# The even layer's gate and convolution products laid between its attentions' steps, and the first transfers and norm reordered

## The reference, cut to what matters

```python
px = hx @ w_in            # 1024 x 4096: eight parts of 512
qa, ka, va, ga, bb, cb, ub, gb = jnp.split(px, 8, axis=-1)
...
# attention over context and tokens, two maps per head, 8 heads of 64
s = jnp.einsum('bqhmd,bkhmd->bhmqk', q, k).astype(jnp.float32) * (A_QK ** -0.5)
p = jax.nn.softmax(s, axis=-1)
a = p[:, :, 0] - lam * p[:, :, 1]
o = jnp.einsum('bhqk,bkhd->bqhd', a, v.astype(jnp.float32))
...
out_a = diff_attention_post(o, subln, lam_init).astype(px.dtype) * jax.nn.silu(ga)
out_b = short_conv(bb, cb, ub, conv_w) * jax.nn.silu(gb)   # bb * conv3(cb * ub)
out_x = jnp.concatenate([out_a, out_b], axis=-1)
...
x = x + g_x * rms_norm(mx @ w_out[l], norm_post[l])
```

## Time and profile before

| | |
|---|---|
| runs | 1628.0 us median of 3 (1619.35 to 1629.15) |
| the profiled execution | 1629.48 us, its span 1627.7 us, mean granted clock 0.949 |
| PE busy | 1428.6 us (88%) |
| PE weight loads busy | 1145.8 us (70%) |
| DVE busy | 743.7 us (46%) |
| ACT busy | 661.2 us (41%) |
| POOL busy | 433.1 us (27%) |

### The profile page before, as it was taken

One profiled execution on the slowest core, in us unless ns is written; L12 is line 12 of the kernel. 1 busy time (PEld: TensorE's weight loads), 2 busy tenths in 40 slices (PEclk: granted clock), 3 DMA queues, 4 the chain that ended last, 5 costly groups with the idle time before them and its releaser, 6 DMA issues. The chain is left out here.

```text
span 1627.7 us, 20847 instructions
## 1 busy us (share of the span) xinstructions
PE 1428.6 (88%) x7788; PEld 1145.8 (70%) x7788; DVE 743.7 (46%) x1455; ACT 661.2 (41%) x1426; POOL 433.1 (27%) x340
## 2 busy tenths in 40 slices
PE   5999789999999788599899879999795898889986
PEld 4777567776787566586677757888684786777765
DVE  2154875644314222604499887322303603982123
ACT  4435226643422333421477662411224423663323
POOL 2433243430343323122100002323131333112522
PEclk9999899999999899799999989999998899999998
DMA  4212242100333534320000001121222210103341
GB/s 160 85 71 78 104 156 78 53 27 27 130 130 128 195 110 149 117 95 35 26 1 1 2 1 52 52 78 53 85 84 107 87 75 26 47 24 138 122 151 56
DMA packets 23250, 129.98 MB, mean 80 GB/s; under 512 B 2544, under 2 KB 4208, under 8 KB 10608
## 3 DMA queue, kind: packets, MB, share of 16 engines
q1 hardware_dynamic: 16304, 106.10, 18.0%
q10 hardware_dynamic: 6848, 22.55, 3.9%
HBM read 122.35 MB, written 6.29 MB: 79 GB/s over the span
## 5 line engine op out<-in xcount | busy, mean ns | idle before, releaser
L930 POOL TENSOR_TENSOR w_low<-w_raw,w_high 128x512 fp32r<-128x512 f32 x296 | 384.6, 1308 | 1112.7 <-ACT w_high L1017 1112.5
L1017 ACT CAST w_high<-w_raw 128x512 fp32r<-128x512 f32 x296 | 179.2, 620 | 667.9 <-PE psum L564 490.8
L564 PE MATMUL psum<-x_high,w_high 128*128 128x512 f32 (+1 forms) x696 | 285.1, 410 | 18.1 <-DVE k_low L1615 8.9
L564 PE MATMUL psum<-x_low,w_high 128*128 128x512 f32 (+1 forms) x696 | 275.0, 395 | 0.0
L564 PE MATMUL psum<-x_high,w_low 128*128 128x512 f32 (+1 forms) x696 | 274.2, 394 | 0.0
L564 PEld LDWEIGHTS psum<-x_high,w_high 128*128 128x128 f32 (+1 forms) x696 | 132.3, 190 | 59.6 <-issue 26.8
L679 PE MATMUL psum<-k_high,q_masked 128*128 128x256 f32 (+3 forms) x512 | 139.2, 356 | 31.4 <-DVE q_masked L1609 15.6
L564 PE MATMUL psum<-w_high,x_high 128*128 128x512 f32 (+1 forms) x352 | 140.5, 399 | 20.0 <-ACT w_high L1017 12.7
L564 PEld LDWEIGHTS psum<-x_high,w_low 128*128 128x128 f32 (+1 forms) x696 | 131.7, 189 | 30.1
L564 PEld LDWEIGHTS psum<-x_low,w_high 128*128 128x128 f32 (+1 forms) x696 | 132.4, 190 | 21.9 <-issue 0.5
L564 PE MATMUL psum<-w_low,x_high 128*128 128x512 f32 (+1 forms) x352 | 137.8, 391 | 0.0
(11 more groups left out here) (262 smaller groups left out, 2468.3 us busy)
## 6 DMA issues: line engine op xcount, KB each, us to landing
w_raw<-stream SPq DMA_DIRECT2D x98, 1024.0 KB, 4.8
x_kept<-arena ACTq DMA_DIRECT2D x8, 512.0 KB, 4.3
arena<-x_kept ACTq DMA_DIRECT2D x8, 512.0 KB, 6.5
arena<-bias ACTq DMA_DIRECT2D x8, 448.0 KB, 3.3
arena<-rows ACTq DMA_DIRECT2D x6, 512.0 KB, 5.3
arena<-x SPq DMA_DIRECT2D x4, 512.0 KB, 5.2
arena<-x ACTq DMA_DIRECT2D x4, 512.0 KB, 6.0
arena<-ctx ACTq DMA_DIRECT2D x4, 512.0 KB, 4.9
```

The source lines that it names most:

```text
L564: mm = pe.matmul(o, l, r, start=(first and n == 0 and kind != "fc"), stop=(last and n == len(passes) - 1))
L930: pool.tensor_tensor(WL[:, u % ROOM, :], RAW[:, g % 2, u % 4, :], WH[:, u % ROOM, :].bitcast(F32), ALU.subtract).then_inc(w_lo, 1)
L1017: act.copy(WH[:, u % ROOM, :], RAW[:, g % 2, u % 4, :]).then_inc(w_hi, 1)
```

## The change

The five chunks e_ga, cb, ub, bb, gc are cut into 20 small ones of two units: 128 output features by the whole depth (`SLIM`; e_gate, e_c, e_u, e_b, e_last, four tiles each, taken tile by tile). `slim` makes such a chunk as 8 pieces of three matmuls on the tokens (bank 6), then 8 on the context (bank 7). PE runs both attentions as one loop over 48 steps (and three to finish), with `feed_even` at four places of each step: after each map's scores, after the first four transposes, and at the end; 320 pieces over 180 feeds, the last at step 44. Transposes now have bank 4 alone, values bank 5. ACT and DVE take each finished part in `fed_even`, one step later: ACT between its two exponentials, DVE between the normalization and its second maximum. ACT copies all transposed tiles, also in "dc". The convolution's output is kept in merge_a's room, the gates in b_high's and b_low's.

After the attentions, ACT and DVE split the six convolution tiles, then DVE squares, takes the reciprocals tile by tile in a new order, and multiplies the gate right behind; then the attention's six tiles are split. The rows of the output weights are rolled, so that the convolution half comes first in eo0. The order of the gate rows, of their transfers and of eo0 is unchanged.

At the start SP sends cols and the identity behind the x tiles, then two granules, then the other constants. ACT waits for cols before the first square and takes one root per tile; DVE scales each tile at once; PE transposes a tile when it comes, over eight banks. ACT's copies of masks and its sigmoid of the condition come after the weights of "keys".

```diff
+SLIM = ("e_gate", "e_c", "e_u", "e_b", "e_last")
...
-    + [("e_q", 8), ("e_k", 8), ("e_v", 8), ("e_ga", 8), ("cb", 8), ("ub", 8), ("bb", 8), ("gc", 8)]
+    + [("e_q", 8), ("e_k", 8), ("e_v", 8)] + [(f"{part}_{j}", 2) for j in range(4) for part in SLIM]
...
+    chunks |= halves("eo", np.roll(a["w_out_2"][0], -512, axis=0)) | halves("oo", a["w_out_2"][1]) | {"dft": dft}
...
+            def slim(chunk):
+                units = UNITS[chunk]
+                for part, x in enumerate((X, C)):
+                    key = (chunk, part)
+                    acc = open_bank(key, 6 + part)
+                    for k in range(NK):
+                        u = units[k // 4]
+                        pe.wait_ge(w_hi, u + 1)
+                        pe.wait_ge(w_lo, u + 1)
+                        w = slice(P * (k % 4), P * (k % 4) + P)
+                        wh, wl = WH[:, u % ROOM, w], WL[:, u % ROOM, w]
+                        hi, lo = x[k]
+                        o = acc[:, 0:hi.shape[-1]]
+                        for n, (l, r) in enumerate(((wh, hi), (wh, lo), (wl, hi))):
+                            mm = pe.matmul(o, l, r, start=k == 0 and n == 0, stop=k == NK - 1 and n == 2)
+                        if k == NK - 1:
+                            fills_bank(mm, key)
+                            closed.append(key)
+                            if part:
+                                unit_done[u] = (bank_full[fills[key][0]], fills[key][1] + 1)
+                        elif part and k == 3:
+                            used[0] += 1
+                            mm.then_inc(w_used, 1)
+                            unit_done[u] = (w_used, used[0])
+                        yield
...
-            pe.wait_ge(sig("consts_in"), 16 * N_CONSTS)
-            pe.wait_ge(sig("xn"), ST)
-            turns("xT", ST, rows_of(A_X), NK)
+            pe.wait_ge(sig("ident_in"), 16)
+            accs = [next_bank(("xT", k)) for k in range(NK)]
+            for t in range(ST):
+                pe.wait_ge(sig("xn"), t + 1)
+                for k in range(NK):
+                    mm = pe.transpose(accs[k][:, P * t:P * t + P], A_X[:, t, P * k:P * k + P], ident)
+                    if t == ST - 1:
+                        fills_bank(mm, ("xT", k))
             gemm("keys", X, ready=turned("xT"))
             gemm("qi", X)
             unit("qa", 0, X)
             unit("qa", 1, X)
+            pe.wait_ge(sig("consts_in"), 16 * N_CONSTS)
...
-            attention("d", keys, *pv)
-            attention("dc", keys, *pv)
-            for i in range(6):
-                pe.wait_ge(sig("sq"), i + 1)
+            def score_two(s, m):
+                name, i = EVEN[s]
+                a = ATT[name]
+                (pr, t), hh = a.duos[i // 2], i % 2
+                scores((name, "S", i, m), score_bank(a, i, m), name, prep_of(name, 2 * pr + hh, m, t), t,
+                       *keys(pr, a.keys(t)))
+            def turn_two(s, c):
+                name, i = EVEN[s]
+                n = ATT[name].keys(0) // P
+                if c >= n:
+                    return
+                pe.wait_ge(sig(f"{name}_p"), i + 1)
+                key = (name, "T", i, c)
+                acc = open_bank(key, 4)
...
+                acc = open_bank(key, 5)
+                for kt in range(n_keys):
+                    for hh in range(2):
+                        mm = pe.matmul(acc[64 * hh:64 * hh + 64, 0:P],
+                                       E_V[:, kt, 64 * (2 * pr + hh):64 * (2 * pr + hh) + 64],
+                                       E_PT[:, 2 * (d % 2) + hh, P * kt:P * kt + P],
+                                       start=kt == 0, stop=kt == n_keys - 1)
+                fills_bank(mm, key)
+            pieces = (piece for j in range(4) for part in SLIM for piece in slim(f"{part}_{j}"))
+            n_pieces, n_feeds = 4 * len(SLIM) * 2 * NK, 4 * (len(EVEN) - 3)
+            def feed_even():
+                n = len(fed["e"])
+                feed("e", pieces, n_pieces * (n + 1) // n_feeds - n_pieces * n // n_feeds if n < n_feeds else 0)
+            for s in range(len(EVEN) + 3):
+                if s < len(EVEN):
+                    score_two(s, 0)
+                feed_even()
+                if s < len(EVEN):
+                    score_two(s, 1)
+                feed_even()
+                if 1 <= s <= len(EVEN):
+                    turn_two(s - 1, 0)
+                feed_even()
+                if 1 <= s <= len(EVEN):
+                    turn_two(s - 1, 4)
+                if s >= 3 and s % 2:
+                    values_two((s - 3) // 2)
+                feed_even()
+            for n, i in enumerate(TILE_ORDER):
+                pe.wait_ge(sig("sq"), n + 1)
                 acc = next_bank(("ms", i))
                 fills_bank(pe.matmul(acc[:, :], square("ones_blk"), E_SQ[:, i, :], start=True, stop=True),
                            ("ms", i))
-            for chunk in ("e_ga", "cb", "ub", "bb", "gc"):
-                gemm(chunk, X, C)
             gate_rows(0)
-            mixed = [(BH[:, k, :], BL[:, k, :]) for k in range(4)] + X[4:]
-            mixed_c = [(KH[:, k, 0:L], KL[:, k, 0:L]) for k in range(4)] + C[4:]
+            mixed, mixed_c = X[4:] + X[:4], C[4:] + C[:4]
             gemm("eo0", mixed, mixed_c, ready=lambda k: pe.wait_ge(sig("mix_lo"), 3 * (k // 2) + 3))
             gemm("eo1", mixed, mixed_c)
...
-            sp.dma_start(SQC[:, :, :], dram["squares"].rearrange("a p n -> p a n")).then_inc(sig("consts_in"), 16)
-            sp.dma_start(COLS[:, :], dram["cols"]).then_inc(sig("consts_in"), 16)
-            sp.dma_start(SEL[:, :], dram["sel"]).then_inc(sig("consts_in"), 16)
-            sp.dma_start(LAM[:, :], dram["lam"].broadcast_to((P, P))).then_inc(sig("consts_in"), 16)
+            sp.dma_start(COLS[:, :], dram["cols"]).then_inc(sig("cols_in"), 16)
+            sp.dma_start(ident, dram["squares"][0]).then_inc(sig("ident_in"), 16)
             for g in range(N_GRANULES):
                 if g == 2:
+                    sp.dma_start(SQC[:, 1:, :], dram["squares"][1:].rearrange("a p n -> p a n")).then_inc(sig("consts_in"), 16)
+                    sp.dma_start(SEL[:, :], dram["sel"]).then_inc(sig("consts_in"), 16)
+                    sp.dma_start(LAM[:, :], dram["lam"].broadcast_to((P, P))).then_inc(sig("consts_in"), 16)
                     sp.dma_start(TAB[:, :, :], dram["tables"][0:2].rearrange("a p n -> p a n")).then_inc(sig("tab_a_in"), 16)
...
+                if t == 0:
+                    act.wait_ge(sig("cols_in"), 16)
+            rms("x", ST, lambda t: A_X[:, t, :], x_ready, A_JUNK, each=True)
...
             ahead("keys")
+            act.wait_ge(sig("consts_in"), 16 * N_CONSTS)
+            for n in range(2):
...
+            def fed_even(s):
+                for chunk, part in closed_in("e", s):
+                    name, j = chunk[:-2], int(chunk[-1])
+                    if name in ("e_gate", "e_last", "e_c"):
+                        ps = filled(act, (chunk, part))[:, 0:L if part else S]
+                    if name == "e_gate":
+                        act.activation((E_GC if part else E_G)[:, j, :], ps, ACT.Sigmoid).then_inc(sig("e_gate_sig"), 1)
+                    if name == "e_last":
+                        if j:
+                            act.wait_ge(sig("e_conv_done"), 2 * j - 1 + part)
+                        act.activation((E_WC if part else E_W)[:, :], ps, ACT.Sigmoid).then_inc(sig("e_last_sig"), 1)
+                    if name == "e_c":
+                        if j:
+                            act.wait_ge(sig("e_conv_in_read"), 2 * j - 1 + part)
+                        frees(act.copy((E_ZC if part else E_Z)[:, :], ps), (chunk, part))
+            for hh in range(2):
+                preps_d(0, hh)
+            for s in range(len(EVEN) + 3):
+                if s:
+                    high((fed["e"] + [fed["e"][-1]] * 8)[4 * s - 1] + ROOM)
+                exps_even(s, 0)
+                if 2 <= s < len(EVEN) + 2:
+                    turned_even(s - 2, 4)
+                if s:
+                    fed_even(s - 1)
+                if 1 <= s <= len(EVEN):
+                    turned_even(s - 1, 0)
+                exps_even(s, 1)
+                if s >= 4 and s % 2 == 0:
+                    values_even((s - 4) // 2)
...
+            act.wait_ge(sig("e_conv_done"), 8)
+            high_mixed([(XH[:, 4 + j, :], E_Y[:, j, :]) for j in range(4)],
+                       [(CH[:, 4 + 2 * p:6 + 2 * p, :], E_YC[:, 2 * p:2 * p + 2, :]) for p in range(2)], lambda n: None)
+            ahead("e_last_3")
...
-            rms("x", ST)
+            dve.wait_ge(sig("cols_in"), 16)
             for t in range(ST):
                 dve.wait_ge(sig(f"x_in{t}"), 16)
+                root_of("x", ST, t)
                 dve.tensor_scalar(A_X[:, t, :], A_X[:, t, :], scr(SSQ + t), None, ALU.mult).then_inc(sig("xn"), 1)
...
+            def convolve(j, z, y, w):
```

(56 more changed lines are left out.)

181 lines of the change are left out of this document (106 added, 75 removed).

## The result

The changed kernel takes 1665.0 us, median of four runs (1662.2 to 1667.8), beside 1627.2 for the kernel before: 1.024 times as long, 95% interval 1.022 to 1.026. The change costs 37.9 us. The forecast was 1646 with a range of 1612 to 1670: the sign and the range hold, the size is about twice what was forecast.

The account below looks back on a forecast made before the run. PE, busy 88% of the span, was taken as the bound, with DVE setting the pace in attention "d". Profiled 1629.5 us, +23.5 for the layer, -5.5 for the start: 1647.5, as a median 1646; range 1612 to 1670.

Parts of the forecast that it names:

- The tail: From the attentions' last copy to the output product: sub-norm reciprocals no longer covered by products, 47.6 us, bounds 43 and 52.
- rival B: After the attentions: the output product starts beneath the reciprocals, four units (16 us) run there, 1630 us; chance 0.07.
- The floor: Attentions with products between their steps: TensorE's own work without any waiting, 313 us.
- probabilities: Attention steps: TensorE waits for probabilities before their transposes, 0.7 us x 18 steps, about 13 us.
- banks: Attention steps: the products' two banks come back late, mostly behind sigmoids and their table loads, 17 us, bounds 0 and 51.
- ripple: Attention steps: the second maximum and second exp queue behind DVE's wait for a sigmoid, 3 us over the run.
- port: Attention steps: POOL's weight splits meet DVE's normalization and slow it, 5 us on TensorE's path, bounds 0 and 36.
- The table loads: Attentions: each of 16 sigmoids costs two loads of 1.28 us, 41 us more on ACT, without a drain gap.
- The start: Kernel's beginning: first product at 19.6 us, a gain of 5.5 us (4 to 7), kept to the end.
- Rival D: Kernel's beginning: it gains nothing because the columns land late, 1651 us; chance given only jointly with the forecast, 0.50.
- A: Attentions: steps pack to TensorE's floor, 321 us, as probabilities and banks return before they are asked for; 1608 us, chance 0.26.
- C: Attentions: DVE and POOL block each other at most steps, or sigmoid steps outlast PE's: +20 to +36, 1666 to 1682; chance 0.15.

## Why the prediction came out as it did

**The tail: right.** 46.9 us against 47.6. Its mechanism was shown twice: without the reciprocals 18 us go (six of 3.35 are 20.1), and with the gate rows behind the output product and the lows earlier 20 go. The sentence that dismissed rival B named the cause of both: the gate rows' four banks.

**The floor and the waits: right, the clock beside them: left out. This is the step that failed.** The sum had 313 for TensorE's work, 38 for waits (13 probabilities, 17 banks, 3 ripple, 5 port) and 8 for the last steps. The trace has 45.8 us idle, of them 7.7 in the last steps (3.70, 1.12, 0.94, 1.17, 0.78): 38.1 for the rest. Of that some 19 for probabilities (26.2 less the last steps' 6.9) where 13, 3 and 5 were meant, and some 16 for banks where 17 were, 12.0 of them at the gates' banks, as forecast. But TensorE was busy for 332.4 us with the same work, 19.4 over the floor. The floor was costed at the full clock throughout, though the sum itself put 38 us of waits into it, and the earlier trace rows already showed 0.85 in "dc" and 0.85 behind the products, where TensorE idles. The term that was missed: 2112 matmuls at a mean granted clock of 0.94. The loss was there to be read: the earlier trace rows has 121.3 + 32.7 + 170.9 = 324.9 us of busy time for the same work, and the sum kept 313 of it (of "dc" 24 for 32.7). So some 12 of the 19.4 us are low clock that the kernel before has too and that the sum let vanish, and some 7.5 came with the change. In one pair of executions 13.1 us less idle time came with 6.9 us less busy time (the sigmoids replaced); how the term follows the waits is not shown beyond that.

**The port: right in size as far as it can be told.** 5 us forecast; with GpSimd's part cut the wait for probabilities was 5.4 us less in one execution, the time 7.6 less, with 2 to 13 possible. The Trainium skill, "SBUF — State Buffer", section "SBUF: two separate sides", has VectorE and GpSimd share one port pair as an exclusive lock, taken by VectorE's operations with two SBUF inputs among others. The groups above agree in that the operation with two SBUF inputs grew, 1159 ns with GpSimd's whole splits beside it against 1018; being means, they do not show the lock itself.

**The table loads: 33 in the attentions, as expected (28 to 33), and without a gap.** The row at 811.43 ends at 812.71 and the sigmoid begins at 812.72. The Trainium skill, "ScalarE: Activation LUTs", section "What ACT_TABLE_LOAD costs", adds a drain to each load; no load here shows one, and the sum did well to go by the row. With the sigmoids replaced 19.8 us went. In the traces 7.3 us of that are waits at the gates' banks, of which the sum had 12, 5.7 are waits for probabilities, and 6.9 are busy time. Whether the probabilities came earlier for ScalarE's time or for the order on it was not separated.

**The start: too large by 2 us at its place, and not kept.** The first product came at 21.75, where 19.6 was forecast. The columns landed as taken (the wait ended at 9.57 where 9.5 was taken). Missed was a second table load: before, the square's table was loaded at 0.74 us, under the wait for the tile; now it stands behind the wait for the columns.

```profile
9.57 1.28 ACT L1151 ACT_TABLE_LOAD   x1 [9.57 <-DMA cols_sb<-cols]
10.87 1.06 ACT L1151 ACTIVATE arena<-arena 128x1024 f32<-128x1024 f32 x1
```

That is 1.3 of the 2.2 us. The larger fault was "kept, as all that follows waits for these products": all that follows also waits for weights, and there were not enough. The profile of before had the wait of 2.45 us at 62.6, and I had not looked at what the start would run into. Rival D, that the start gains nothing, holds for the time in all, though not for its reason: the columns were in time.

**The rivals.** A (packs to the floor) fell: it needed attentions under 325 us, and they took 378.3, and 350.7 even with three causes of waiting cut. B (the output product under the reciprocals) fell by the wait of 27.8 us, for the reason given against it. C (VectorE and GpSimd block each other at most steps, or sigmoid steps outlast TensorE's) fell as a mechanism, though its time, 1666 to 1682, begins 1 us above the result: the blocking is some 5 us on the path, and the waits at the gates' banks are what the forecast had. I had no case for "the waits as forecast, and the clock behind them". That the result lies in the stated range is owed to the room left for C, not to the sum. A slip without effect: with the banks at their bound the terms add up to 393, not 395.

**What stays open.** What, beside the wait itself, decides whether the low clock follows: at one place and with nearly the same wait it came in one run and not in another. So the clock's share in an edit's gain is partly chance, and the edits' gains in the attentions were taken from one profiled execution each; two executions of one kernel here differ by up to 10 us.

## What to carry to other kernels

Where a sum of costs puts single waits of microseconds into TensorE's work, look in the rows at the clock behind such waits and cost the work there by it, or take the busy time of the same work as it was measured, low clock included; here the full-clock floor was 19 us short. Before products are laid between other work to fill its idle time, ask what they covered where they stood: here 20 us of reciprocals came into the open. And when an engine stands still for data, look whether it is a bank that it lacks: the gate rows behind the output product's first half, with their transfers issued early, were worth 12.8 us in the kernel before, where the interleaving with all its repairs won nothing. And a gain at the start lasted here only when the first wait for weights behind it was taken out too.
